# Dilated attention and output projection as one program: last head in the order 4, 16, 1, its dilation-1 result copied on chip

## The reference, cut to what matters

```python
for window, dil in ((128, 1), (512, 4), (2048, 16)):          # prompt: 2048 tokens, 8 heads x 64
    o, l = _dilated_prompt_cfg(qa, ka, va, rel_bias, window, dil)   # softmax(q k^T/8 + bias) v over 129 keys
    outs.append(o); lses.append(l)
attn = _combine_by_denominator(outs, lses)                     # softmax over the 3 log denominators
...
a_out = attn.reshape(B, T, D_A) * jax.nn.silu(ga)
o_n = o_b * lax.rsqrt(jnp.mean(jnp.square(o_b), -1, keepdims=True) + NORM_EPS) * norm_g
b_out = o_n.reshape(B, T, D_B) * jax.nn.silu(gb)
z = ALPHA * x + jnp.concatenate([a_out, b_out], -1) @ w_out    # (2048 + 64 rows) x 1024, by 1024 x 1024
y = layer_norm(z) * ln_g + ln_b
```

## Time and profile before

| | us |
|---|---|
| runs of the kernel before | 1623.42, 1624.63, 5037.28 |
| their median | 1624.63 |
| the profiled execution | 1627.94 |
| its span from first to last instruction | 1626.1 |
| PE busy in the span | 1535.0 (94%) |
| DVE / ACT / POOL busy | 766.0 / 503.4 / 450.0 |
| mean granted TensorE clock | 0.958 of full |

### The profile page before, as it was taken

How to read it: one execution, slowest core, us unless ns; L and a number is a source line. 1 busy time by engine, 2 the same in 40 slices (tenths; PEclk the granted TensorE clock), 3 DMA queues, 4 the chain that set the end, 5 groups by cost and what they waited for, 6 DMA issues and landing times. The chain is left out here.

```text
span 1626.1 us, 25533 instructions
## 1 busy us (share of the span) xinstructions
PE 1535.0 (94%) x9806; PEld 1373.7 (84%) x9806; DVE 766.0 (47%) x1941; ACT 503.4 (31%) x1425; POOL 450.0 (28%) x264
## 2 busy tenths in 40 slices
PE   7999999997899998999997999978999999599998
PEld 7999999994678776777785999978999999378886
DVE  6022110004232214222113799846777777488885
ACT  5111111112100113222213032335777777322321
POOL 1233300000150000000001000019797678445553
PEclk9999999997999999999998599989999999799999
DMA  9999996235865867967556347869698962856642
GB/s 300 336 328 343 348 297 174 79 124 161 262 179 148 320 223 250 298 209 235 191 176 160 88 156 231 250 196 203 132 203 182 198 165 75 275 189 225 231 158 78
DMA packets 176581, 340.50 MB, mean 209 GB/s; under 512 B 15667, under 2 KB 115315, under 8 KB 167603
## 3 DMA queue, kind: packets, MB, share of 16 engines
q1 hardware_dynamic: 144572, 173.44, 34.7%
q10 hardware_dynamic: 21392, 109.19, 21.0%
q0 software_dynamic: 10512, 56.48, 13.4%
HBM read 263.34 MB, written 156.48 MB: 258 GB/s over the span
## 5 line engine op out<-in xcount | busy, mean ns | idle before, releaser
L254 PE MATMUL acc<-xhi,whi 128*128 128x424 f32 (+1 forms) x640 | 227.7, 356 | 8.8 <-DVE xlo L233 8.8
L743 PE MATMUL nacc<-nwhi,nxhi 128*128 128x512 f32 (+1 forms) x544 | 220.2, 405 | 9.2 <-DVE nwlo L492 9.2
L254 PE MATMUL acc<-xlo,whi 128*128 128x424 f32 (+1 forms) x640 | 227.2, 355 | 0.0
L254 PE MATMUL acc<-xhi,wlo 128*128 128x424 f32 (+1 forms) x640 | 227.0, 355 | 0.0
L743 PE MATMUL nacc<-nwhi,nxlo 128*128 128x512 f32 (+1 forms) x544 | 215.4, 396 | 0.0
L743 PE MATMUL nacc<-nwlo,nxhi 128*128 128x512 f32 (+1 forms) x544 | 215.4, 396 | 0.0
L1344 ACT ACTIVATE a_prob<-a_prob,a_stage 128x256 f32<-128x256 f32 (+1 forms) x384 | 174.1, 454 | 88.2 <-DVE a_stage L1320 85.7
L1260 POOL CAST a_sorted<-a_plain 128x2048 fp32r<-128x2048 f32 x48 | 183.0, 3868 | 38.3 <-PE a_s_ps L1380 38.3
L1320 DVE CUSTOM_DVE_ANT_0 a_prob<-a_s_ps,a_bias 128x256 f32<-128x256 f32 (+1 forms) x384 | 125.4, 364 | 83.9 <-issue 62.9
L1404 PE MATMUL a_o_ps<-a_v,a_probT 128*128 128x64 f32 x1200 | 158.0, 270 | 0.2
L1404 PEld LDWEIGHTS a_o_ps<-a_v,a_probT 128*128 128x128 f32 x1200 | 150.2, 193 | 2.3 <-DVE a_probT L1331 1.6
(11 more groups left out here) (196 smaller groups left out, 2536.7 us busy)
## 6 DMA issues: line engine op xcount, KB each, us to landing
a_plain<-split_qk POOLq DMA_DIRECT2D x48, 512.0 KB, 11.3
out_kwin_s<-in_cache_kT ACTq DMA_DIRECT2D x8, 2048.0 KB, 19.8
split_qk<-spare POOLq DMA_DIRECT2D x16, 1024.0 KB, 14.4
spare<-in_xT SPq DMA_DIRECT2D x32, 512.0 KB, 7.6
projN<-nstage SPq DMA_DIRECT2D x32, 512.0 KB, 5.5
qg<-in_cache_kT ACTq DMA_DIRECT2D x8, 2048.0 KB, 10.9
d_vlow<-in_cache_v ACTq DMA_DIRECT2D x8, 2048.0 KB
out_kwin_s<-in_cache_kT ACTq DMA_DIRECT2D x8, 2032.0 KB, 29.5
```

Of the source, the lines that this page charges most:

```text
L254: mm = pe.matmul(acc[:, j, 0:n], w[:, u, k], x[:, k, c0:c0 + n], start=(k == 0 and a == 0), stop=(k == KD - 1 and a == 2))
L743: mm = pe.matmul(acc[0:m, n % 2], x[:, u, k, 0:m], w[:, k, g * H:(g + 1) * H], start=(k == 0 and b == 0), stop=(k == KD - 1 and b == 2))
```

## The change

The two stages become one function, `attend_and_project`, with one Block, so each engine runs from its attention list straight into that of the last stage.

- The units are numbered through eight halves (`h`); the last half takes its dilations in the order 4, 16, 1 (`ORDER`). Its sorted keys go to other places: dilation 4 over `plain[0]`, dilation 16 over the first sorted buffer, each copied one step earlier than by the old rule.
- The last pair's dilation-1 result is not stored. `load_partials` loads six heads of dilation 1 from HBM, and POOL copies the other two from `stage` (`own_heads`, once for each tile, 132 numbers in each partition).
- The samples' mixture (tile 0) is made inside the last half: squares on ACT after unit 168, mean and gates on POOL among the weight splits, `combine(0)` on DVE at unit 188, `recurrent_part(0)` on ACT after unit 191, and `transposes(0)` on PE between the products of unit 188 and the transposes of unit 191.
- DVE then runs `rest_of_mix(0)`, `weigh(1)`, `combine(1)`: the remainder of tile 0 no longer stands behind `weigh(1)`.
- SP issues the gates of tiles 1 to 3 (`load_gates`) as soon as seven weight pieces are split, and then the partials. The weights go to other places (pieces 0 to 2 to the second sorted buffer, 3 to 5 to `plain[0]`, 6 and 7 to `m_late_w`), each under its own wait.
- The last stage's buffers are laid over attention buffers that are free by then; all of PSUM is one tensor, `a_banks`. Waits are the same in attention, written without offsets; one semaphore increment of DVE for each unit goes.

```diff
+    HALVES, PER = 2 * NG, NBK // 2
+    ORDER = [(0, 1, 2)] * (HALVES - 1) + [(1, 2, 0)]
+    units = [(h, c, b) for h in range(HALVES) for c in ORDER[h] for b in range(0, NBK, 2)]
+    HU = PER * NC
+    NU = len(units)
...
+    def done(h, c):
+
+        return HU * h + PER * (ORDER[h].index(c) + 1)
...
+        mt_ps, z_ps = (banks[:, 2:4], banks[:, 6:8]), (banks[:, 4:6], banks[:, 0:2])
...
@@ sync
-                    if g == NG - 1:
-                        sp.wait_ge(pv_done, NU * g + 3)
...
-                        for k in range(5):
-                            load_weights(k)
-                    for c, d in enumerate(DILS):
-                        if g == NG - 1 and c == 1:
-                            for k in range(5, KD):
-                                load_weights(k)
...
+                def load_gates(p):
+                    u, rows = (p - 1) % 3, slice(row0_of[p], row0_of[p] + P)
+                    sp.dma_start(ob[u], o_b[rows, :]).then_inc(m_landed[u], 16)
+                    sp.dma_start(gate[:, u].rearrange("p g d -> p (g d)"), projN[rows, 2 * WA:4 * WA]).then_inc(m_landed[u], 16)
+
+                def load_partials(p):
+                    u, rows = (p - 1) % 3, slice(row0_of[p], row0_of[p] + P)
+                    sp.dma_start(pt[:, u, 1:3], partials[1:3, rows, :, :].rearrange("c p h w -> p c h w")).then_inc(m_landed[u], 16)
+                    sp.dma_start(pt[:, u, 0, 0:HA - 2], partials[0, rows, 0:HA - 2, :]).then_inc(m_landed[u], 16)
...
+                for k in range(4):
+                    load_weights(k)
+                store_partials(NG - 1, 1)
+                for k in range(4, 7):
+                    load_weights(k)
+                store_partials(NG - 1, 2)
+                load_weights(7)
+                sp.wait_ge(pv_done, done(HALVES - 1, 2))
+                sp.wait_ge(w_lo, 7)
+                for p in (1, 2, 3):
+                    load_gates(p)
+                sp.wait_ge(stage_free[0], 64 * (NG - 1))
+                for c in (1, 2):
+                    sp.wait_ge(stage_free[c], 64 * NG)
+                load_partials(1)
+                load_x(0)
+                load_partials(2)
@@ gpsimd
+                    if h == HALVES - 1:
+                        dst = plain[0] if c == 1 else sorted_[0]
+                        pool.wait_ge(s_done, done(h - 1, 0 if c == 1 else 1))
...
+                def own_heads(p):
+                    pool.wait_ge(o_out, done(HALVES - 1, 2) // 4 + (p - 1) // 8 + 1)
+                    if p >= 4:
+                        pool.wait_ge(mix_done, p - 2)
+                    nc.gpsimd.tensor_copy(pt[:, (p - 1) % 3, 0, HA - 2:HA], stage[:, 0, p - 1]).then_inc(own_done, 1)
...
+                pool.wait_ge(s_done, done(HALVES - 2, 2))
+                for k in range(0, 3):
+                    split_weights(k)
+                pool.wait_ge(sq_done, HB)
...
+                gated(0)
+                pool.wait_ge(s_done, done(HALVES - 1, 1))
+                for k in range(3, 6):
+                    split_weights(k)
+                pool.wait_ge(s_done, done(HALVES - 1, 2))
+                for k in range(6, KD):
+                    split_weights(k)
+                own_heads(1)
+                gated(1)
@@ vector
-                combine(0)
-                for i in range(LAST + 2):
+                for n in range(NU + 3):
+                    if n < NU:
+                        lowest(n)
+                    if n >= 3:
+                        turned(n - 3)
+                    if n == NU - 4:
+                        combine(0)
+                rest_of_mix(0)
+                weigh(1)
+                combine(1)
+                for i in range(1, LAST + 2):
@@ scalar
+                    if n == HU * (HALVES - 1):
+                        sample_squares()
+                    if n == NU - 1:
+                        recurrent_part(0)
+                    if n == NU + 3:
+                        round_mix(0)
@@ tensor
-                transposes(0)
+                for n in range(NU + 4):
+                    if n < NU:
+                        scores(n)
+                    if n == NU + 1:
+                        transposes(0)
+                    if 2 <= n < NU + 2:
+                        turn(n - 2)
+                    if n >= 4:
+                        values(n - 4)
                 for p in range(LAST):
                     project(p)
```

More of the change, by code:

```diff
@@ L1208, in _ @@
             def _(sp):
[L1209 to L1213, removed]
                 def load_weights(k):
@@ new lines, in store_partials @@
+                def store_partials(g, c):
+                    d = DILS[c]
+                    sp.wait_ge(o_out, done(2 * g + 1, c) // 4)
+                    rows = partials[c, :, 2 * g:2 * g + 2, :].rearrange("(j p r) h w -> p r j (h w)", p=P, r=d)
+                    src = stage[:, c].rearrange("p (r j) h w -> p r j (h w)", r=d)
+                    if c == 1:
+                        for j in range(NBK // d):
+                            sp.dma_start(rows[:, :, j], src[:, :, j]).then_inc(stage_free[c], 16)
+                    else:
+                        a, b = (rows[:, 0], src[:, 0]) if d == 1 else (rows[:, :, 0], src[:, :, 0])
+                        for half in range(4):
+                            m = NBK // 4
+                            sp.dma_start(a[:, half * m:(half + 1) * m], b[:, half * m:(half + 1) * m]
+                                         ).then_inc(stage_free[c], 16)
@@ new lines, in _ @@
+                load_x(1)
+                load_partials(3)
+                load_x(2)
+                for p in range(1, NALL):
+                    if p + 3 < NALL:
+                        sp.wait_ge(mix_done, p + 1)
+                        sp.wait_ge(b_done, p + 1)
+                        load_partials(p + 3)
+                        load_gates(p + 3)
+                    if p >= 2 and p + 1 < NALL:
+                        sp.wait_ge(zr, p - 1)
+                        load_x(p + 1)
+                    if p >= 3:
+                        store(p - 3)
@@ L1250, in _, with sort @@
+                for p in range(NALL - 3, LAST):
+                    store(p)
+                sp.wait_ge(last_y, 1)
+                sp.dma_start(y[row0_of[LAST]:row0_of[LAST] + P, 0:H], yt[:, LAST % 2, 0:H]).then_inc(y_free[LAST % 2], 16)
+                sp.wait_ge(copied, 32 * 2 * NB)
+                sp.wait_ge(y_free[0], 16 * (NTL // 2 + 2))
+                sp.wait_ge(y_free[1], 16 * (NTL // 2))
             @block.gpsimd
             def _(pool):
-                def sort(g, x, c):
-                    half, d = 2 * g + x, DILS[c]
+                def sort(h, c):
+                    g, x = divmod(h, 2)
+                    src, dst, d = plain[x], sorted_[c - 1], DILS[c]
@@ L1639, in combine @@
                         wait_inputs(dve, 0)
-                        tt(a, first["mix"][0:n], g[:, 0:H], ALU.mult).then_inc(mix_done, 1)
+                        dve.wait_ge(s_done, done(HALVES - 1, 2))
+                        tt(a, first_mix, g[:, 0:H], ALU.mult).then_inc(mix_done, 1)
                         return
```

619 lines of the change are left out of this document (280 added, 339 removed).

## The result

| | median, us | runs, us | ratio to before, 95% interval |
|---|---|---|---|
| before, on the same chip | 1624.03 | 1623.33 to 5037.28 (4) | |
| after | 1643.7 | 1641.49 to 1644.96 (4) | 1.0121 (1.0101 to 1.0141) |

What follows compares the result with a forecast made beforehand. PE was taken as the bound, so only its hole before the projection could shrink: transposes of tile 1 10.3 us earlier, less 2.7 of slow clock, 7.6 saved from the 1624.63 median gives 1617.0 us, range 1607 to 1624.5.

Steps and rivals of the forecast that it cites:

- The hole and its edges: Between attention and projection PE has 20.7 us of silence and 2.7 of slow clock; 12.6 us of hole would remain.
- SP's and POOL's chain from dilation 4 on: Last half: store of dilation 4 at 1372.2, then weight pieces and splits, the last split by 1392.3, then gates.
- The sorts: Sorted keys for the last half's new dilation order are ready in time, so nothing waits and the reorder costs nothing.
- Landing and mixture of tile 1: At the seam, tile 1's data land at 1403.0 and its mixture, 6.8 us later, is ready at 1409.8.
- the slow clock behind it: After the remaining hole the clock has fallen again, costing about 2.7 us behind tile 1's transposes.
- From the trace to the runs: The saving of 7.6 us, read in the profiled 1627.94 us execution, was taken off the runs' median of 1624.63.
- The copies of own heads add 0: In the last stage, POOL's copy of 0.3 us a tile costs DVE at most 1.04, within its room: 0 added.
- a stage where PE is the bound: In the last stage, one store less and one more DMA for each tile change nothing, as PE sets the time.
- 1.6 us of room in a tile of 12: Last stage: DVE's remainder ends at 1521.41 and PE uses it at 1522.97, so DVE could absorb the copies.
- A longer tile (copies): Sign of a wrong forecast: a last-stage tile takes longer than 12.0 us because of POOL's copies.
- the last stage is paced by DVE: Rival, chance 0.03: copies exceed DVE's 1.6 us of room; 16 tiles at 0.6 us more eat the gain, 1627.
- it needs 2.2 us a tile: Last stage: the copies must cost DVE 2.2 us in each tile before DVE paces it.

Runs made afterwards that it cites:

- exp_before_scale: The changed kernel, POOL copy kept, with ACT's exponentials of tile i+1 ahead of its scaling of tile i-2: 1621.55 us, ratio 0.998 to before.
- copy_on_act: The changed kernel with the copy of the pair's own two heads made on ACT instead of POOL: 1635.91 us, ratio 1.0067 to before.

## Why the prediction was wrong

- *The hole and its edges*: right. It held a wait for loads and the fall of the clock, and PE ran from the last products into tile 0's projection without a pause.
- *SP's and POOL's chain from dilation 4 on*: right to 1 us at each of its steps. The sorts held nothing up. One wait that I didn't have, 1.3 us of PE at 1355.1 for ACT's exponentials, comes with the samples' squares, which now stand in ACT's list there (four of them between 1352.4 and 1354.1). It didn't delay the end of attention: the projection started at 1391.45, where I had 1391.6.
- *Landing and mixture of tile 1*: the mechanism right, two terms too small, 2.1 us for the landing and, beside POOL's gate products, a stretch of 2.1 in `weigh(1)` where I had 1.0 in the sums. (The same step takes 1.13 at 1406.54 in the trace of before; I had read only the 1.65.) So PE resumed 3.4 us late, and the slow clock behind it cost 1.5 us instead of 2.7: the seam gave 5.5 of 7.6 against that trace.
- *From the trace to the runs*: I took the 7.6 us off the runs' median, though they were read in an execution 3.3 us above it, and the profiles of the other kernels put the excess at the seam. Against ordinary executions the seam gave about 2 us; with the last stage healthy, the change gains about 3 us of whole time (exp_before_scale).
- *The copies of own heads add 0*, and "a stage where PE is the bound": this is the step that failed, and it turned the sign. I set 0.3 us against "1.6 us of room in a tile of 12", as if each tile had that room anew. It was a stock, how early the remainder is ready, and is used up once. It would be there anew only if DVE began each tile at a wait for PE. It never did (0.1 us of idle at L1660 in 28), so what the copy costs adds up, and the lag grew by 0.2 a tile. The failure is the room and not only the copy's price: with the copy off POOL the kernel still tips and is 0.7% slower than before (copy_on_act), since PE's tile got shorter and DVE's didn't. "A longer tile (copies)" stood among my signs of being wrong, and it came. I also weighed only the copy against DVE and left out POOL's addition, which comes at PE's beat while DVE's sums come at DVE's. The rule that the prediction took from the Trainium skill (SBUF — State Buffer, Who interferes with whom), that whoever issues first gets the shared pair of ports for its whole instruction, was the right one, and the traces agree: 0.03 us ahead, DVE's sum took 0.69; 0.01 behind, 2.93. I applied it to the new instruction's length, and it had to be applied to the order of all that meet.
- *The rival "the last stage is paced by DVE"* (0.03) named the right place, wait and sign. Its price was wrong: "it needs 2.2 us a tile". 0.1 to 0.2 us a tile was enough, and what it then costs is 2.1 us in each tile left. A cost of this kind doesn't grow with its cause: the copy on POOL cost 14 us in the old kernel, 8 in the changed one (1643.7 against 1635.91), which tips without it too, and nothing at all where DVE's loop had 0.7 us of idle.

What stays open: why PE's tile takes 12.01 us in the changed kernel and 12.07 in the kernel before. The traces say where: the six matmuls of a weight piece take 1.40 or 1.41 us, but in the changed kernel those of pieces 3 and 5, which now lie in `plain[0]`, take 1.36 to 1.37 (1437.17 to 1438.54, 1428.79 to 1430.15), and those of piece 4, behind the transposes, 1.46 instead of 1.48. Whether the place of the weights does it wasn't tried, nor was the old order of the last pair's dilations with the rest of the change kept.

## What to carry to other kernels

Before you say that a side engine has room, compare periods: follow one of its instructions and one of the bounding engine's over ten tiles, and look whether the side engine ever waits for the bounding one. If it doesn't, what room there is gets used up once, and any addition adds up until something tips. Where instructions of two engines hold each other up and each engine has its own pace, look who starts first and by how much. And put a short instruction that another engine waits for ahead of a long one that nobody does: here that cost nothing and gave the whole loop its slack.

## What the hardware showed that I hadn't expected

- A stage with two lasting tempos, 12.0 and 14.3 us a tile, and 0.01 us of order between them.
- A DVE sum of two SBUF operands that starts just behind POOL's 2.4 us addition takes 2.7 to 2.9 us instead of 0.69. DVE's addition of the input, with one operand in PSUM, takes its 1.28 for two beside POOL's addition (L1546 at 1457.81) and 1.27 with POOL's already over (1472.15).
- POOL's copy of 132 numbers took 0.29 us at 1464.92 and 1479.25 and up to 1.91 elsewhere, so its recorded time is mostly waiting. The one at 1452.87 ended 0.15 us behind DVE's product of `weigh` on two SBUF operands, which had started ahead of it (1452.72 to 1454.48).
